# FFN output projection on Trainium2: three of four block sums in each group made by accumulating DMAs on GpSimd's queue

## The reference

```
gate, up = c[..., :D_FF], c[..., D_FF:]                               # c: 256 x 11264
return (jax.nn.gelu(gate, approximate=True) * up) @ w_ffn_out         # w_ffn_out: 5632 x 2048, fp32
...
x = x + rmsnorm(conv_gated_ffn(...), g_ffn_post[l])
```

## Time and profile before

| | before |
|---|---|
| median of 3 runs | 1800.8 us |
| the profiled execution: its time / its span | 1801.42 us / 1799.7 us |
| TensorE busy (matmul) | 1786.6 us, 99% |
| VectorE busy | 1138.0 us, 63% |
| ScalarE busy | 944.2 us, 52% |
| GpSimd busy | 64.0 us, 4% |
| DMA moved, mean rate | 330.74 MB, 184 GB/s |
| granted TensorE clock, mean | 0.999 of full |

### The profile page before, as it was taken

How to read it: one execution, slowest core, us unless ns; L and a number is a source line. 1 busy time by engine, 2 the same in 40 slices (tenths; PEclk the granted TensorE clock), 3 DMA queues, 4 the chain that set the end, 5 groups by cost and what they waited for, 6 DMA issues and landing times.

```text
span 1799.7 us, 24906 instructions
## 1 busy us (share of the span) xinstructions
PE 1786.6 (99%) x8694; PEld 1492.7 (83%) x8694; DVE 1138.0 (63%) x1588; ACT 944.2 (52%) x1287; POOL 64.0 (4%) x132
## 2 busy tenths in 40 slices
PE   9999999999999999999999999999999999999998
PEld 7888888888888888888888878888888888888786
DVE  5554555555456554444444477777777777788887
ACT  7555566665545655544544464444444444455554
POOL 4000000000000110000000100000000000000002
PEclk9999999999999999999999999999999999999999
DMA  8455544455566555555434546555555555556565
GB/s 286 152 187 175 168 161 147 156 173 164 171 226 219 202 187 179 172 186 188 141 139 163 187 164 234 187 186 186 186 186 186 186 186 186 197 164 205 194 197 189
DMA packets 167021, 330.74 MB, mean 184 GB/s; under 512 B 8454, under 2 KB 14006, under 8 KB 165558
## 3 DMA queue, kind: packets, MB, share of 16 engines
q1 hardware_dynamic: 165414, 318.48, 53.6%
q10 hardware_dynamic: 1552, 11.54, 1.6%
HBM read 325.81 MB, written 4.19 MB: 183 GB/s over the span
## 4 chain that ended last, share of the span: by engine, by line
PE 98%; DVE 1%; ACT 1%; DMA 0%; issue 0%; DVEq 0%; ACTq 0%
PE bank L564 17%; PE bank L566 17%; PE bank L970 17%; PE bank L565 17%; PE bank L972 9%; PE bank L1018 4%; PE bank L1019 4%; PE bank L1020 4%; PE bank L596 1%; PE bank L880 1%; PE bank L897 1%; PE bank L763 1%; PE bank L762 1%; PE bank L779 0%; PE bank L770 0%; DVE actA L1882 0%
## 5 line engine op out<-in xcount | busy, mean ns | idle before, releaser
L1582 DVE TENSOR_TENSOR wlo<-raw,whi 128x1024 fp32r<-128x1024 f32 x520 | 641.2, 1235 | 577.2 <-ACT whi L1129 450.2
L1129 ACT ACTIVATE whi<-raw 128x1024 fp32r<-128x1024 f32 x400 | 423.9, 1060 | 514.3 <-PE bank L566 304.6
L970 PE MATMUL bank<-actA,whi 128*128 128x512 f32 x1344 | 472.0, 394 | 0.0
L972 PE MATMUL bank<-actA,wlo 128*128 128x256 f32 x1344 | 380.1, 283 | 0.0
L970 PEld LDWEIGHTS bank<-actA,whi 128*128 128x128 f32 x1344 | 252.4, 188 | 58.3
L564 PE MATMUL bank<-whi,actA 128*128 128x512 f32 x672 | 274.8, 409 | 1.3 <-DVE wlo L1582 0.5
L566 PE MATMUL bank<-whi,actA 128*128 128x512 f32 x672 | 265.3, 395 | 0.0
L565 PE MATMUL bank<-wlo,actA 128*128 128x512 f32 x672 | 265.0, 394 | 0.0
L972 PEld LDWEIGHTS bank<-actA,wlo 128*128 128x128 f32 x1344 | 252.7, 188 | 0.0
L564 PE MATMUL bank<-whi,actB 128*128 128x512 f32 x576 | 229.4, 398 | 0.0
L566 PE MATMUL bank<-whi,actB 128*128 128x512 f32 x576 | 227.5, 395 | 0.0
(11 more groups left out here) (262 smaller groups left out, 1812.7 us busy)
## 6 DMA issues: line engine op xcount, KB each, us to landing
raw<-in_w_ffn_in SPq DMA_DIRECT2D x88, 1024.0 KB
raw<-in_w_in SPq DMA_DIRECT2D x48, 1024.0 KB
raw<-in_w_ffn_out SPq DMA_DIRECT2D x84, 512.0 KB, 4.9
raw<-in_w_mem_kv SPq DMA_DIRECT2D x32, 1024.0 KB
raw<-in_w_attn_br SPq DMA_DIRECT2D x16, 1024.0 KB
raw<-in_w_mix_out SPq DMA_DIRECT2D x16, 1024.0 KB
raw<-in_w_mem_q SPq DMA_DIRECT2D x16, 1024.0 KB
raw<-in_w_mem_o SPq DMA_DIRECT2D x16, 1024.0 KB
```

The lines of the kernel that those rows point to most:

```text
L970: pe.matmul(dst[:, :], whi[:, s, o:o + P], actA[:, :, kt, :], start=(kt == 0), stop=False)
L972: mm = pe.matmul(dst[:, 0:S], wlo[:, s, o:o + P], actA[:, 0, kt, :], start=False, stop=(kt == KD - 1))
L1129: act.activation(whi[:, ks % AHEAD, 0:w], raw[:, c, ks % 2, 0:w], ACT.Copy).then_inc(hi_done, 1)
L1582: dve.tensor_tensor(wlo[:, vs % AHEAD, 0:w], raw[:, c, vs % 2, 0:w], f32(whi[:, vs % AHEAD, 0:w]), ALU.subtract).then_inc(lo_done, 1)
```

## The change

Of the four sums of a group only f7 is still made by VectorE. The other three are made in place in `raw` by DMAs that GpSimd issues with `accum_op=ALU.add`: they read a block of w_ffn_out from HBM and add it to what the half slot holds. Four of them make three sums, since f6 is built in two steps in w22's half slot (first + w12, called "half6", then + w11). In a group GpSimd issues, in this order: half6 (after the low part of unit w22 is made), f4 (after that of w11), f5 (after w12 has landed) and f6 (after half6 has landed). ScalarE waits for the DMA of its unit (`w_added`). To suit this the order of the formed units becomes w22, w11, w21, f5, f4, f6, f7 (except in group (1, 0), which still opens with w11), and w12 is loaded six units before f5.

```
-    FORMS = ("w11", "w22", "f4", "w21", "f5", "f6", "f7")
-    BRINGS = {"w11": "w11", "w22": "w22", "f4": "w12", "w21": "w21"}
-    SUMS = ("f4", "f5", "f6", "f7")
+    FORMS = ("w22", "w11", "w21", "f5", "f4", "f6", "f7")
+    BRINGS = {"w11": "w11", "w22": "w22", "f5": "w12", "w21": "w21"}
+    F5_LEAD = 6
+    FORMS_1 = ("w11", "w22", "w21", "f5", "f4", "f6", "f7")
...
+        def accumulate(to, what, f):
+
+            p, g = to[0:2]
+            pool.dma_start(rawb(to).rearrange("p (k n) -> p k n", n=NC), in_hbm(p, g, what),
+                           accum_op=ALU.add).then_inc(w_added[f], 16)
+
+        for n, (p, g, f) in enumerate(FOUT):
+            here, top, left = (p, g, "w22"), (p, g, "w12"), (p, g, "w11")
+            if f == "w11":
+                pool.wait_ge(lo_done, V_FOUT + FOUT.index((p, g, "w22")) + 1)
+                accumulate(here, "w12", "half6")
+                pool.wait_ge(lo_done, V_FOUT + n + 1)
+                accumulate(left, "w12", "f4")
+                pool.wait_ge(b_loaded[HOME[top]], LANDED[top])
+                accumulate(top, "w22", "f5")
+                pool.wait_ge(w_added["half6"], 16 * (p * G0 + g + 1))
+                accumulate(here, "w11", "f6")
         post(N_Y3, y3, gpost3, 2, ND - 1)
...
-                if FOUT[n] == (0, 0, "w11"):
+                if FOUT[n] == (0, 0, "w22"):
                     pe.wait_ge(uconv, 2 * NF)
-                if FOUT[n] == (0, 0, "w22"):
                     pe.wait_ge(xs_lo, 4)
...
-            if u[2] in SUMS:
+            if u[2] == "f7":
                 act.wait_ge(f_added, SUM_OF[u] + 1)
+            elif u[2] in w_added:
+                act.wait_ge(w_added[u[2]], 16 * (u[0] * G0 + u[1] + 1))
             else:
                 act.wait_ge(b_loaded[HOME[u]], LANDED[u])
...
-            w11, w12, w21, w22 = (rawb((p, g, b)) for b in ("w11", "w12", "w21", "w22"))
-            if f == "f4":
-                dve.wait_ge(b_loaded[HOME[p, g, "w12"]], LANDED[p, g, "w12"])
-                op = dve.tensor_tensor(w11, w11, w12, ALU.add)
-            elif f == "f5":
-                op = dve.tensor_tensor(w12, w12, w22, ALU.add)
-            elif f == "f6":
-                op = dve.tensor_tensor(w11, w11, w22, ALU.add)
-            else:
-                dve.wait_ge(f_added, SUM_OF[p, g, "f6"] + 1)
-                op = dve.tensor_tensor(w21, w21, w11, ALU.add)
-            op.then_inc(f_added, 1)
+            w21 = rawb((p, g, "w21"))
+            dve.wait_ge(w_added["f6"], 16 * (p * G0 + g + 1))
+            dve.tensor_tensor(w21, w21, rawb((p, g, "w22")), ALU.add).then_inc(f_added, 1)
```

More of the change, by code:

```diff
@@ L81, in hybrid_layer @@
     G0, G1 = 3, 4
-    FORMS = ("w11", "w22", "f4", "w21", "f5", "f6", "f7")
-    BRINGS = {"w11": "w11", "w22": "w22", "f4": "w12", "w21": "w21"}
-    SUMS = ("f4", "f5", "f6", "f7")
+    FORMS = ("w22", "w11", "w21", "f5", "f4", "f6", "f7")
+    BRINGS = {"w11": "w11", "w22": "w22", "f5": "w12", "w21": "w21"}
+    F5_LEAD = 6
+    FORMS_1 = ("w11", "w22", "w21", "f5", "f4", "f6", "f7")
     SUM_LEAD = 6
     def pair_units(p, groups, kinds):
-        forms = iter([(p, g, f) for g in range(groups) for f in FORMS])
+        forms = iter([(p, g, f) for g in range(groups) for f in (FORMS_1 if (p, g) == (1, 0) else FORMS)])
         plain = iter([(p, k, c) for c in range(2) for k in range(2 * groups, KF // 2)])
@@ L302, in hybrid_layer @@
     b_loaded = [sem(f"b_loaded{h}") for h in range(2 * RAW_SLOTS)]
+    w_added = {f: sem(f"{f}_added") for f in ("half6", "f4", "f5", "f6")}
     f_added, xs_step, xs_full, xs_hi, xs_lo, q_copied, y_step = (sem(n) for n in (
@@ L347, in hybrid_layer @@
     B11, B21, B12, B22, Q1, Q6, Q5, Q7 = 0, 1, 4, 5, 2, 3, 6, 7
-    SUM_OF = {(u[0], u[1], u[2]): n for n, u in enumerate(sorted(
-        (u for u in FOUT if u[2] in SUMS), key=FOUT.index))}
+    SUM_OF = {u: n for n, u in enumerate(u for u in FOUT if u[2] == "f7")}
     def released(b):
         p, g, f = b
-        if f == "w11":
+        if f == "w22" and FOUT.index((p, g, "f7")) - SUM_LEAD >= FOUT.index((p, g, "f6")) - AHEAD:
             return "added", SUM_OF[p, g, "f7"] + 1
-        if f == "w22":
-            return "added", SUM_OF[p, g, "f6"] + 1
-        return "low", V_FOUT + FOUT.index((p, g, {"w12": "f5", "w21": "f7"}.get(f, f))) + 1
+        last = {"w11": "f4", "w12": "f5", "w22": "f6", "w21": "f7"}.get(f, f)
+        return "low", V_FOUT + FOUT.index((p, g, last)) + 1
     def released_at(b):
@@ L380, in hybrid_layer @@
         HOME[b], LANDED[b] = h, 16 * loads[h]
+        for f in {"w11": ("f4",), "w12": ("f5",), "w22": ("half6", "f6")}.get(b[2], ()):
+            HOME[b[0], b[1], f] = h
     for n in range(4):
@@ L389, in form_at, with in_hbm @@
         p, g, f = u
-        return rawb((p, g, {"f4": "w11", "f6": "w11", "f5": "w12", "f7": "w21"}.get(f, f)))
+        return rawb((p, g, {"f4": "w11", "f6": "w22", "f5": "w12", "f7": "w21"}.get(f, f)))
+    w_out = rows("w_ffn_out")
+    def in_hbm(p, g, f):
+        if f == 0 or f == 1:
+            k, c = 2 * g, 2 * p + f
+        else:
+            k, c = 4 * g + 2 * (f in ("w21", "w22")), 2 * p + (f in ("w12", "w22"))
+        return w_out[:, k:k + 2, c * NC:(c + 1) * NC]
     block = ctx.enter_context(nc.Block())
@@ L457, in _ @@
                 column(V_FIN // 2 + 8 * i + 4 * m, rows("w_ffn_in"), i * NC + m * DFF)
-        w_out = rows("w_ffn_out")
         for j in range(2):
@@ L463, in block_load @@
         def block_load(b):
-            p, g, f = b
-            if f == 0 or f == 1:
-                k, c = 2 * g, 2 * p + f
-            else:
-                k, c = 4 * g + 2 * (f in ("w21", "w22")), 2 * p + (f in ("w12", "w22"))
             kind, n = FREE[b]
@@ L2098, in combine @@
             op.then_inc(y_step, 1)
-        for n in range(4, SUM_LEAD):
-            if FOUT[n][2] in SUMS:
-                f_add(n)
         for n in range(NU):
@@ L2105, in _ @@
                 f_lo_of(n + AHEAD)
-            if n + SUM_LEAD < NU and FOUT[n + SUM_LEAD][2] in SUMS:
+            if n + SUM_LEAD < NU and FOUT[n + SUM_LEAD][2] == "f7":
                 f_add(n + SUM_LEAD)
```

6 lines of the change are left out of this document (2 added, 4 removed).

## The result

| | before | after |
|---|---|---|
| median (4 runs each) | 1801.0 us | 1858.1 us (1856.9 to 1859.3) |
| the profiled execution: its time / its span | 1801.42 / 1799.7 us | 1857.81 / 1856.1 us |
| granted TensorE clock, mean | 0.999 | 0.987 |
| data moved by GpSimd's queue | 0 | 14.68 MB in 28 DMAs |

The change makes the kernel slower: 1.0317 times the time before, 95% interval 1.0304 to 1.033. That is 57.1 us against the 27.6 us of the forecast, inside the range.

What follows compares the result with a forecast made beforehand. TensorE, busy 99% of the span, was taken as the bound. Added waits of 3.4 + 5 x 4.1 + 3.9 = 27.8 us on the profiled 1801.4 gave 1829.2, as a median 1828.6 us (+1.5%); range 1803.5 to 1862.

Steps and rivals of the forecast that it cites:

- What it removes: FFN output stage: 21 sums, 25.6 us of VectorE's time, go; TensorE waited for none, so worth 0.
- First added wait: Before unit 17, moved up from unit 19: TensorE stands still once for the last activation sum, 3.4 us.
- Second added wait: Before f5: ready 10.3 us after a 6.2 us window opens, 4.1 us late in five groups; group (0, 0) spared.
- half6 is not in the way there: GpSimd's queue ahead of f4 and f5: half6 goes out 4.2 us earlier and its data ends after 4.1 us.
- Group (1, 0): half6, f4 and f5 start together there: need 12.9 us in a 9.0 us window, so f5 3.9 us late.
- The data price: Data of one accumulated block on the DMA engines: 2.6 us taken, two reads, bounded by 1.3 and 3.9 us.
- Cheap accumulation: Rival: issue about 0.4 us, second read free, f5 ready in 5.3 us; only +3.4 left, 1804.2 us; chance 0.17.
- In between: Rival: data as a plain load, uncovered issues of 1.5 us; f5 0.4 to 1.7 late, about 1810 us; chance 0.15.
- Heavy accumulation: Rival: 3.9 us of data each, f5 6.7 us late five times, DMA the bound; +44.7, 1845.5 us; chance 0.14.
- VectorE holds GpSimd up: Rival: each GpSimd issue waits out a VectorE instruction, 6 x 1.2 = 7.4 us more, 1836 us; chance 0.06.
- The clock falls: Rival: TensorE's clock halves after each f5 stall for about as long as the stall, +12, 1841 us; chance 0.07.
- A gain: Rival: VectorE, near full, paced the matmuls; worth at most 0.4 us and what missing matmuls hide; chance 0.03.

Runs made afterwards that it cites:

- the last kernel above: Changed kernel with f5 issued before f4, half6 dropped, f6 made by VectorE, last activation sum one step earlier, full computation: 1802.2 us, ratio 1.001.
- the kernel without the chain: Changed kernel with f5 issued early and half6 put into w12's half slot, so f6 follows no other accumulation; sums not the reference's: 1814.2 us, ratio 1.0076.

## Why the prediction was wrong

- **What it removes: 0.** Right. VectorE's time fell by 23.1 us (forecast 25.6), and in the last kernel above, where all that was added is hidden, the time is not below that of before.
- **First added wait: 3.4 us.** Right in place and size (3.37). It falls on unit 17, released by VectorE's sum; group (1, 3) has none.
- **Second added wait: f5, in six groups, (0, 0) spared.** Right in place: the six stalls are before f5, and none is in group (0, 0). The size was off: 24.4 us forecast in the six groups, 37.7 measured, 13 us more. This is the **first step that failed**: f5's need from the opening of the window, 10.3 us in the forecast, was 13.0 in group (0, 1). Term by term, from the packet counts above:

| term of f5's need, group (0, 1) | forecast | measured |
|---|---|---|
| until f4's data begins | 1.5 (f4's issue) | 2.7 (half6's data ends then) |
| data of f4 | 2.6 | 3.5 |
| data of f5, with a plain load beside it | 2.6 + 1.3 | 4.7 |
| from there until ScalarE starts | 2.3 | 2.1 |

The assumption "half6 is not in the way there" failed: its data was to be through 4.1 us after its issue, and took 6.9. Two plain loads' worth of packets (542 on SyncE's queue) moved beside it, where the forecast had none. Leaving half6 out gives only 0.7 us back in this group, since f4's own start of 1.9 us then takes the place of the 2.7. The rest is the price of the data itself: 8.2 us for f4, f5 and the load beside them, in place of 6.5. How the load and the accumulations slow each other is not separated. The landings tell the same: 7.6 to 9.1 us for f4 and 11.0 to 12.3 for f5 in the six groups, where 6 to 8 had been named for both.
- **Group (1, 0): 3.9 us late.** Measured 5.4, and 1.0 without half6, so that its three accumulations in one window were rightly seen.
- **The data price.** I took two reads, 2.6 us; the queue's row gives 3.1, and plain copies on the same queue 1.6. The ratio is 2.0. The rule of the Trainium skill's "Collectives: The Full Stack" (The bandwidth ceiling), that a reduce runs at half the rate of a copy because it reads two sources, agrees with the ratio. The figure was short because a plain copy on this queue already takes 1.6 us and not the 1.3 that I had worked out from the full stretches. That two reads are the reason is not shown: the row gives the time and twice the packets, not what they do.
- **Cheap accumulation (0.17).** Fell: plain copies alone give 1817.0. An estimate from the formula of the Trainium skill's "DMA: Bandwidth & Descriptors" (Anatomy of one DMA, SWDGE path), 2.0 us plus bytes over 436 GB/s, has a block there after 3.2 us; the fastest accumulation took 6.0 us and the fastest plain copy 4.4. The measurement decides against it here, with other loads on the same engines.
- **In between (0.15).** Fell: the issue is near its 1.5 us, but the data is not that of a plain load, and no f5 stall of the six is under 5.2 us.
- **Heavy accumulation (0.14).** Its time of 1845.5 was the nearest of the cases with stalls alone, but its data price of 3.9 us was 3.1, and its reason, DMA as the bound, is contradicted: the kernel without the chain moves the same packets in 1814.2.
- **VectorE holds GpSimd up (0.06).** Fell: an issue that stands alone takes 1.19 to 1.21 us while VectorE is at work (the first of all 1.34). Only the second and third issues in direct succession take longer, 1.7 and 2.2 us.
- **The clock falls (0.07).** This is the **second step that failed**. I put a stall of 4.1 us "just short" of the 4.5 us seen at the end and left the clock out of the sum. That row is of a tail with no matmul after it; the runs show that 3.4 us can suffice, in another kernel 1.9, that a wait of 3.3 need not, and that each stall of 5 us and more did. It is 15.3 us of the 56.4, and with the 13 us above it makes the whole difference to the forecast (3.4 + 37.7 + 15.3). The 12 us of the rival were near the mark, in part by luck, since the slow stretch is not as long as the stall before it; its chance was set too low.
- **A gain (0.03).** Fell: 23.1 us less on VectorE bought nothing.

What stays open: what decides whether a short wait lowers the clock; how an accumulation and a plain load slow each other on the engines; and why a plain copy on GpSimd's queue, with 1.6 us of data and 0.72 us of issue, still needs 6.7 us in the median, with a load on SyncE's at 4.9.

## What to carry to other kernels

A DMA that accumulates is slow here and lands late: before one replaces an instruction of an engine that is not the bound, ask who waits for it, what stands ahead of it in its one queue, and whether it needs the landing of another. With the same bytes and packets, another order and chain gave back 44 of the 57 us; in the old order, copies at half the engine time gave back 41. Full DMA engines alone say little: they were as full through a group in which TensorE never waited. And after any stall of TensorE of some microseconds, count the slow matmuls that follow it: here they were a quarter of the loss.

## What had not been expected of the hardware

- The granted clock fell after an idle time of 3.4 us, and the matmuls stayed at half clock for 2.7 to 5.7 us after each of the seven stalls. Idle time and the slow stretch behind it are not in proportion: it was 5.7 us after a wait of 6.5, and 4.0 after one of 6.8. In other kernels it fell after 1.9 us and stayed full after 3.3.
- An accumulation of 512 KB on GpSimd's queue took twice the engine time of a copy (3.1 against 1.6 us), nearly twice the packets (7616 against 4032 for 28 DMAs), and 1.20 against 0.72 us for its issue.
- With the DMA engines 0.97 busy through a group, TensorE waited 6.9 us in one kernel and not at all in another.
- The landing of an accumulation spreads from 6.0 to 12.3 us in the same stage, and with f5 first f6 waited for one landing (half6, 8.9 us) and then needed its own (9.8 us).
